# Weights ring of a four-stage transformer trunk: three buffers of 2 MB or six of 1 MB

## Chip, cores, metric

One NeuronCore of a Trainium2 chip runs the whole kernel as one program. The metric is the device time of one execution in microseconds, the median of several. TensorE multiplies; VectorE (DVE), ScalarE (ACT), GpSimd (POOL) and SyncE (SP) work beside it, each with an instruction stream of its own, tied together by semaphores.

## What is computed

Two decoder layers over 256 tokens of width 1024, all in float32. Each layer mixes tokens (a combined input projection, compressed, selected and windowed attention, a short convolution, a retention branch, gates and an output projection) and then mixes channels, with a layer norm after each:

```
for l in range(2):
    x = layer_norm(ALPHA * x + token_mixer(x, ...), ln1_g[l], ln1_b[l])
    f = swiglu(x, ffn_gate, ffn_up, ffn_down) if l == 0 else moe_swiglu(x, router, moe_gate, moe_up, moe_down)
    x = layer_norm(ALPHA * x + f, ln2_g[l], ln2_b[l])

swiglu(x, g, u, d) = (silu(x @ g) * (x @ u)) @ d        # 1024 -> 3584 -> 1024
moe_swiglu: top 2 of 8 experts for each token, softmax over the two logits, each expert a swiglu
```

Every weight is used once per execution, so some 493 MB of them pass through the core.

## The kernel before

**The stream of weights.** The host cuts all large weights into subs of 128 partitions x 2048 floats (1 MB) in the order of their use: 46 subs for a mixer, 42 for the dense layer, 46 for the second mixer and 42 for each of eight experts, 470 in all. Two neighbouring subs make a tile of 2 MB, in which each partition's row of 16 KB is contiguous. `NTILES` is 235. The ring `raw` has `RING` = 3 slots of one tile each. SP fills it (lines 276 to 309): the first three tiles at the start, the constants behind the first, then each tile t when `lo_done` has reached 2t - 4, which is when VectorE has split sub 2t - 5, the second half of the tile that had the slot. One more tile, that nobody reads, is loaded at the end.

**The split.** A float32 product is made of three passes with the shorter type fp32r. ScalarE's `split` (line 823) waits until the tile has landed (`landed`, one semaphore for each slot, only before the even sub) and until TensorE has used the sub three before (`sub_used`), and rounds the sub into `w_hi`, a ring of three subs. VectorE's `split` (line 1114) waits for it and writes the rest, raw - w_hi, to `w_lo` (line 1117) and counts `lo_done`. TensorE waits for `lo_done` of a sub before it multiplies with it. So raw is free after VectorE's split.

**The stages.** Mixers and dense layer run with 256 tokens; their matmuls are recorded at lines 329 to 331 and 343 to 345. For the experts the tokens of one expert are gathered into 128 slots by a matmul with a selection matrix (line 716), and outputs are scattered back (lines 785, 786) and added with the weights on VectorE (line 1589, `add_scattered`). A loop runs over items; an item is an expert, with an extra item for an expert that has more than 128 tokens. In this run there are eight. An item has 42 subs: two for the first gate block, and then per block of 512 hidden channels two for `up`, two for the next `gate`, two for `down` (the last block has no next gate). `body` in each engine's `experts` is one block of six subs, in which each engine has its instructions between the splits by a fixed hand-written order: TensorE multiplies `up`, half of the next gate, makes the four transposes of `hidden` (line 742), multiplies the other half and `down`; ScalarE applies silu (line 1039) and copies the transposed hidden (`hidden_block`, line 1043); VectorE multiplies silu by up (line 1565) and writes its lower part `act_lo` (`lower`, line 1569) between two splits. TensorE's `down` waits for that lower part.

The queue of an engine is in order: a split that waits for its weights holds up all that stands behind it on ScalarE, and through `hi_done` what stands behind the split on VectorE. SP's queue holds only the loads. The norms' parameters (1 MB, line 849, `load_norm`) are loaded by ScalarE's queue.

Of the kernel before, what the change touches and what calls it, by code (L numbers as in the profile page):

```python
# [23 lines left out]
ACT = mybir.ActivationFunctionType  # L24
# [3 lines left out]
P = 128  # L28
D = 1024
# [3 lines left out]
DK = D // P  # L33
# [12 lines left out]
NE = 8  # L46
# [11 lines left out]
LAYER = MIX + FFN  # L58
MOE0 = LAYER + MIX
RING = 3  # L60
NEXT = (0, MIX, LAYER, MOE0)
NTILES = (MOE0 + NE * FFN) // 2
ITEM_TILES = FFN // 2


PA = (0, 1)
# [67 lines left out]
def trunk(nc, wstream, x, consts, constb, small, ln, router, out):  # L134
    with ExitStack() as ctx:
# [4 lines left out]
            return ctx.enter_context(nc.semaphore(name))  # L140


        raw = sb("raw", [P, RING, 2 * SUB])
        w_hi = sb("w_hi", [P, RING, SUB], F32R)
        w_lo = sb("w_lo", [P, RING, SUB], F32R)
        xT_hi = sb("xT_hi", [P, DK, T], F32R)
# [81 lines left out]
        logT = rg[0:NE, 0, :]  # L228


        landed = [sem(f"landed{i}") for i in range(RING)]
        hi_done, lo_done = sem("hi_done"), sem("lo_done")
        sub_used = sem("sub_used")
        half_unit = sem("half_unit")
# [25 lines left out]
            sem(n) for n in ("esilu_rdy", "ehid_rdy", "et_ps", "ehT_hi", "ehT_rdy", "y_hi_rdy", "y_rdy", "scat_ps", "acc_rdy"))  # L260
        act_chain, dve_chain = sem("act_chain"), sem("dve_chain")

        def wait_landed(eng, sub):

            tile = sub // 2
            eng.wait_ge(landed[tile % RING], 16 * (tile // RING + 1))

        def raw_half(slot, half):
            return raw[:, slot, half * SUB:(half + 1) * SUB]

        block = ctx.enter_context(nc.Block())


        @block.sync
        def _(sp):
            sp.dma_start(X[:, :, :], x.rearrange("(t p) d -> p t d", p=P)).then_inc(x_in, 16)
            sp.dma_start(ident, consts[:, C_ID:C_ID + P]).then_inc(x_in, 16)
            for t in range(RING):
                sp.dma_start(raw[:, t], wstream[t]).then_inc(landed[t], 16)
                if t == 0:  # L280
                    sp.dma_start(cst[:, P:C_W], consts[:, P:C_W]).then_inc(const_in, 16)
                    sp.dma_start(cstf, constb).then_inc(const_in, 16)
                    sp.dma_start(sm[:, :, :], small.rearrange("l p c -> p l c")).then_inc(const_in, 16)
            rest = NTILES - RING

            def tile(slot, src, index):

                sp.wait_ge(lo_done, 2 * index - 2 * RING + 2)
                sp.dma_start(raw[:, slot], src).then_inc(landed[slot], 16)

            with sp.Fori(0, rest // RING) as i:
                for c in range(RING):
                    t = i * RING + (RING + c)
                    tile(c, wstream[bass.ds(t, 1)].rearrange("a p c -> (a p) c"), t)
            for t in range(RING + rest // RING * RING, NTILES):
                tile(t % RING, wstream[t], t)

            sp.wait_ge(table_rdy, 1)
            extra = sp.value_load(table[0:1, NX:NX + 1], min_val=0, max_val=NX)
            with sp.If(extra > 0):  # L300
                with sp.Fori(0, extra) as i:
                    e = sp.value_load(table[0:1, bass.ds(i, 1)], min_val=0, max_val=NE - 1)
                    with sp.Fori(0, ITEM_TILES // RING) as b:
                        for c in range(RING):
                            t = e * ITEM_TILES + b * RING + (MOE0 // 2 + c)
                            tile((NTILES + c) % RING, wstream[bass.ds(t, 1)].rearrange("a p c -> (a p) c"),
                                 i * ITEM_TILES + b * RING + (NTILES + c))

            tile(NTILES % RING, wstream[0], extra * ITEM_TILES + NTILES)


        @block.tensor
# [506 lines left out]
        def _(act):  # L819
# [2 lines left out]

            def split(at, k=0):

                if at % 2 == 0:
                    act.wait_ge(landed[at // 2 % RING], (k + (at // 6 + 1)) * 16)
                if at >= RING:
                    act.wait_ge(sub_used, k * 6 + (at - RING + 1))
                activate(w_hi[:, at % RING], raw_half(at // 2 % RING, at % 2), ACT.Copy).then_inc(hi_done, 1)  # L829

            def norm(n):

# [277 lines left out]
        def _(dve):  # L1110
# [3 lines left out]
            def split(at, k=0):  # L1114

                dve.wait_ge(hi_done, k * 6 + (at + 1))
                v.tensor_tensor(w_lo[:, at % RING], raw_half(at // 2 % RING, at % 2), w_hi[:, at % RING],  # L1117
                                ALU.subtract).then_inc(lo_done, 1)

            def add_x(n, t, c):  # L1120
# [524 lines left out]
def host_layout(a):  # L1645

    def rows(w, k):
        return w.reshape(k, P, -1).transpose(1, 0, 2)

    def cut(w, k):  # L1650
        w = rows(w, k)
        n = w.shape[2] // 256
        return w.reshape(P, k, n, 256).transpose(2, 0, 1, 3).reshape(n, P, SUB)

    subs = []
    for l in range(L):
        w = a["w_in"][l]
        q, kv, ng, rest = w[:, :512], w[:, 512:1280], w[:, 1280:1304], w[:, 1304:]
        ngp = np.zeros((D, 256), np.float32)
        ngp[:, :24] = ng  # L1660
        conv_b, conv_c, conv_h = rest[:, :512], rest[:, 512:1024], rest[:, 1024:1536]
        ret, mg = rest[:, 1536:3584], rest[:, 3584:].reshape(D, 3, D)
        first = list(cut(np.concatenate([q, kv, ngp], 1), DK))
        subs += first[:4]
        for kv_ in range(2):
            w1 = a["cmp_w1"][l, kv_].reshape(16, P, CH)
            for h in range(2):
                subs.append(w1[8 * h:8 * h + 8].transpose(1, 0, 2).reshape(P, SUB))
        subs += first[4:]
        subs += list(cut(np.concatenate([conv_c, conv_h, conv_b, ret], 1), DK))  # L1670
        for b in (1, 0, 2):
            g = cut(mg[:, b], DK)
            br = [rows(a["w_br"][l, b][:, c * 512:(c + 1) * 512], 4).reshape(P, SUB) for c in range(2)]
            subs += [g[0], g[1], br[0], g[2], g[3], br[1]]
        for c in range(2):
            wo = rows(a["w_out"][l][:, c * 512:(c + 1) * 512], DK)
            subs += [wo[:, 4 * h:4 * h + 4].reshape(P, SUB) for h in range(2)]
        if l == 0:
            gate, up, down = a["ffn_gate"][0], a["ffn_up"][0], a["ffn_down"][0]
            g, u = cut(gate, DK), cut(up, DK)  # L1680
            d = down.reshape(2 * NB, 2, P, D).transpose(0, 2, 1, 3).reshape(2 * NB, P, SUB)
            subs += [g[0], g[1]]
            for b in range(NB):
                subs += [u[2 * b], u[2 * b + 1]]
                if b + 1 < NB:
                    subs += [g[2 * b + 2], g[2 * b + 3]]
                subs += [d[2 * b], d[2 * b + 1]]
    head = np.stack(subs).reshape(-1, 2, P, SUB).transpose(0, 2, 1, 3).reshape(-1, P, 2 * SUB)
    stream = np.empty((NTILES, P, 2 * SUB), np.float32)
    stream[:len(head)] = head  # L1690
    assert len(head) == MOE0 // 2
    t = len(head)

    def wide(w):
        return rows(w, DK).reshape(P, DK, NB, 512).transpose(2, 0, 1, 3).reshape(NB, P, 2 * SUB)
    for e in range(NE):
        g, u = wide(a["moe_gate"][0, e]), wide(a["moe_up"][0, e])
        d = a["moe_down"][0, e].reshape(NB, 4, P, D).transpose(0, 2, 1, 3).reshape(NB, P, 2 * SUB)
        stream[t] = g[0]
        t += 1  # L1700
        for b in range(NB):
            stream[t] = u[b]
            t += 1
            if b + 1 < NB:
                stream[t] = g[b + 1]
                t += 1
            stream[t] = d[b]
            t += 1
    assert t == NTILES

    small = np.zeros((L, P, S_W), np.float32)
    for l in range(L):
        s = small[l]
        for kv in range(2):
            s[:, S_POS + kv * P:S_POS + kv * P + 16] = a["cmp_pos"][l, kv].reshape(16, P).T
        s[:, S_B1:S_B1 + 4] = a["cmp_b1"][l].reshape(4, P).T
        w2 = a["cmp_w2"][l].reshape(2, 2, P, DH)
        for c in range(2):
            s[:, S_W2K + c * P:S_W2K + c * P + DH] = w2[0, c]
            s[:, S_W2K + c * P + DH:S_W2K + (c + 1) * P] = w2[0, c]  # L1720
            s[:, S_W2V + c * DH:S_W2V + (c + 1) * DH] = w2[1, c]
        s[:DH, S_B2K] = a["cmp_b2"][l, 0]
        s[DH:, S_B2K] = a["cmp_b2"][l, 0]
        s[:, S_CONV:S_CONV + 12] = a["conv_w"][l].reshape(12, P).T
        s[:, S_GNG:S_GNG + 4] = a["ret_gn_g"][l].reshape(4, P).T
        s[:, S_GNB:S_GNB + 4] = a["ret_gn_b"][l].reshape(4, P).T
        s[0, S_B2V:S_B2V + DH] = a["cmp_b2"][l, 1]
    ln = np.stack([np.stack([a[f"ln{n}_g"][l], a[f"ln{n}_b"][l]]) for l in range(L) for n in (1, 2)])
    router = np.zeros((P, DK, P), np.float32)
    router[:, :, :NE] = rows(a["moe_router"][0], DK)  # L1730
    return stream, small, ln, router
# [49 lines left out]
```

## Time and profile before

| | us |
|---|---|
| median of 3 runs | 1923.12 (1921.77 to 1929.84) |
| profiled execution, its own time | 1928.55 |
| its span, first to last instruction | 1926.7 |
| TensorE busy | 1870.9 (97%) |
| VectorE busy | 1429.5 (74%) |
| ScalarE busy | 1131.1 (59%) |
| weights' loads, 236 of 2048 KB, median from issue to landing | 8.9 |

The profile is of one execution. Busy time of TensorE overlaps, since matmuls are pipelined: a matmul of 512 columns is recorded with 0.39 us while the next starts 0.23 us after it. "Idle before" and a wait name the instruction that ended the idle time. In a table of stretches, DMA is the mean busy share of the core's 16 DMA engines in the stretch and GB/s what they moved. Time from issue to landing counts from the instruction on the issuing queue to the last of 16 completions.

### The profile page before, as it was taken

How to read it: one execution, taken by the hardware profiler on the slowest of the kernel's cores; microseconds unless marked ns; L12 is line 12 of the kernel's file. 1: busy time of each engine (PE TensorE's matmuls, PEld its weight loads, DVE VectorE, ACT ScalarE, POOL GpSimd, SP SyncE). 2: the span in 40 equal slices, each digit the busy share in tenths (PEclk: the TensorE clock that was granted, in tenths of full speed). 3: DMA queues.
4: the chain of work that ended last, by engine and by line, in shares of the span. 5: the costliest groups of instructions: out<-in, count | busy, mean ns of one | idle time of the engine just before them, and what ended most of it. 6: DMA issues, size and time to landing. Idle time of an engine off the chain costs nothing.

```text
span 1926.7 us, 28135 instructions
## 1 busy us (share of the span) xinstructions
PE 1870.9 (97%) x11156; PEld 1630.9 (85%) x11160; DVE 1429.5 (74%) x1214; ACT 1131.1 (59%) x972; POOL 0.2 (0%) x4
## 2 busy tenths in 40 slices
PE   7999999999999999999999999999999999999996
PEld 7999998999979999996888888887887887888885
DVE  4585577444565575668888889888888898888987
ACT  5444344443435445435777777777777777776774
POOL 0000000000000000000000000000000000000000
PEclk9999999999999999999999999999999999999998
DMA  8543434554436443454998999989989899899893
GB/s 327 182 167 133 154 140 188 181 202 185 174 131 224 153 149 132 154 186 153 353 364 329 359 345 354 368 321 360 361 327 367 328 363 362 318 366 366 333 369 153
DMA packets 36026, 504.68 MB, mean 262 GB/s; under 512 B 3968, under 2 KB 4096, under 8 KB 5248
## 3 DMA queue, kind: packets, MB, share of 16 engines
q1 hardware_dynamic: 34960, 498.06, 68.9%
q10 hardware_dynamic: 1008, 5.77, 0.8%
q8 instruction: 46, 0.75, 0.2%
q14 instruction: 12, 0.10, 0.0%
HBM read 502.76 MB, written 1.05 MB: 261 GB/s over the span
## 4 chain that ended last, share of the span: by engine, by line
PE 65%; DMA 14%; DVE 10%; ACT 6%; issue 5%; SPq 0%; DVEq 0%; ACTq 0%
DMA raw<-wstream 14%; PE PS L329 10%; PE PS L330 10%; PE PS L331 10%; PE PS L343 9%; PE PS L345 9%; PE PS L344 9%; DVE w_lo L1117 5%; ACT w_hi L829 5%; PE PS L483 1%; PE PS L716 1%; PE PS L742 1%; PE PS L515 1%; DVE act_lo L1569 1%; PE PS L498 1%
## 5 line engine op out<-in xcount | busy, mean ns | idle before, releaser
L1117 DVE TENSOR_TENSOR w_lo<-raw,w_hi 128x2048 fp32r<-128x2048 f32 x472 | 1076.9, 2289 | 346.8 <-ACT w_hi L829 346.2
L829 ACT ACTIVATE w_hi<-raw 128x2048 fp32r<-128x2048 f32 x472 | 902.2, 1915 | 360.0 <-PE PS L345 188.7
L329 PE MATMUL PS<-xT_hi,w_hi 128*128 128x256 f32 x1456 | 421.3, 289 | 10.8 <-DVE w_lo L1117 5.6
L330 PE MATMUL PS<-xT_lo,w_hi 128*128 128x256 f32 x1456 | 414.4, 285 | 0.0
L331 PE MATMUL PS<-xT_hi,w_lo 128*128 128x256 f32 x1456 | 414.2, 284 | 0.0
L343 PE MATMUL PS<-w_hi,xT_hi 128*128 128x512 f32 x896 | 355.1, 396 | 2.6 <-DVE xT_lo L1555 1.5
L345 PE MATMUL PS<-w_hi,xT_lo 128*128 128x512 f32 x896 | 349.6, 390 | 0.0
L344 PE MATMUL PS<-w_lo,xT_hi 128*128 128x512 f32 x896 | 349.0, 390 | 0.0
L329 PEld LDWEIGHTS PS<-xT_hi,w_hi 128*128 128x128 f32 x1456 | 281.8, 194 | 22.7 <-issue 19.7
L330 PEld LDWEIGHTS PS<-xT_lo,w_hi 128*128 128x128 f32 x1456 | 281.9, 194 | 0.2
L331 PEld LDWEIGHTS PS<-xT_hi,w_lo 128*128 128x128 f32 x1456 | 281.7, 193 | 0.0
L343 PE MATMUL PS<-w_hi,act_hi 128*128 128x512 f32 x624 | 246.1, 394 | 12.4 <-DVE act_lo L1569 10.1
L345 PE MATMUL PS<-w_hi,act_lo 128*128 128x512 f32 x624 | 243.1, 390 | 0.0
L344 PE MATMUL PS<-w_lo,act_hi 128*128 128x512 f32 x624 | 243.1, 390 | 0.0
L343 PEld LDWEIGHTS PS<-w_hi,xT_hi 128*128 128x128 f32 x896 | 168.3, 188 | 39.2 <-DVE w_lo L1117 4.5
L345 PEld LDWEIGHTS PS<-w_hi,xT_lo 128*128 128x128 f32 x896 | 168.2, 188 | 35.9
L344 PEld LDWEIGHTS PS<-w_lo,xT_hi 128*128 128x128 f32 x896 | 168.4, 188 | 33.2
L343 PEld LDWEIGHTS PS<-w_hi,act_hi 128*128 128x128 f32 x624 | 117.1, 188 | 45.5 <-DVE w_lo L1117 14.4
L345 PEld LDWEIGHTS PS<-w_hi,act_lo 128*128 128x128 f32 x624 | 117.1, 188 | 24.7
L344 PEld LDWEIGHTS PS<-w_lo,act_hi 128*128 128x128 f32 x624 | 117.2, 188 | 23.3
L911 ACT ACTIVATE G<-PS 128x512 f32<-128x512 f32 x24 | 14.3, 597 | 77.5 <-PE PS L331 40.2
L329 PE MATMUL PS<-act_hi,w_hi 128*128 128x256 f32 x192 | 55.2, 288 | 0.0
(248 smaller groups left out, 1355.1 us busy)
## 6 DMA issues: line engine op xcount, KB each, us to landing
raw<-wstream SPq DMA_DIRECT2D x236, 2048.0 KB, 8.9
soft<-ln ACTq DMA_DIRECT2D x4, 1024.0 KB, 6.5
X<-x SPq DMA_DIRECT2D x1, 1024.0 KB, 4.9
out<-X ACTq DMA_DIRECT2D x2, 512.0 KB, 2.7
cst<-consts SPq DMA_DIRECT2D x1, 890.5 KB, 10.7
sm<-small SPq DMA_DIRECT2D x1, 729.0 KB, 12.5
bufA<-router ACTq DMA_DIRECT2D x1, 512.0 KB, 3.8
rg<-constb SPq DMA_DIRECT2D x1, 335.0 KB, 11.1
```

Source lines behind the costliest of these rows:

```text
L329: mm(o, wh, rhs_hi[:, k, :], start=(k == 0), stop=False)
L330: mm(o, wh, rhs_lo[:, k, :], start=False, stop=False)
L331: last = mm(o, wl, rhs_hi[:, k, :], start=False, stop=(k == nk - 1))
L343: mm(o, lh, wh, start=(first and n == 0), stop=False)
L344: mm(o, lh, wl, start=False, stop=False)
L345: last = mm(o, ll, wh, start=False, stop=(final and n == len(ks) - 1))
L483: last = mm(o[par][:, i, 0:w], query(NR * g + 2 * i + par, qt), kT[par * DH:(par + 1) * DH, a, g, 0:w], start=False, stop=(i == 1), skip_g ...
L498: last = nc.tensor.transpose(PS[:, TB + kb, r * P:(r + 1) * P], prob[:, r, kb * P:(kb + 1) * P], ident)
L515: last = mm(o[par], V[:, a, kb, g * DH:(g + 1) * DH], probT[:, kb * 512 + par * 256:kb * 512 + (par + 1) * 256], start=(a == 0 and kb == 0 ...
L716: last = mm(PS[:, TB + k // 4, (k % 4) * P:(k % 4 + 1) * P], X[:, t, k * P:(k + 1) * P], pick[:, t, :], start=(t == 0), stop=(t == TT - 1))
L829: activate(w_hi[:, at % RING], raw_half(at // 2 % RING, at % 2), ACT.Copy).then_inc(hi_done, 1)
L1117: v.tensor_tensor(w_lo[:, at % RING], raw_half(at // 2 % RING, at % 2), w_hi[:, at % RING], ALU.subtract).then_inc(lo_done, 1)
```

## The change

`raw` becomes a ring of `RAW` = 6 slots of one sub (the same 48 KB of each partition). The host's stream is laid out by subs, each with contiguous rows of 8 KB. SP loads each sub by itself, sub s when `lo_done` has reached s - 5, which is when VectorE has split sub s - 6. The first six subs are loaded at the start, with the constants behind the second. There are six `landed` semaphores, and ScalarE waits for one before each sub. Two subs, not one tile, are loaded at the end for nobody. For the experts the halves of each block are cut so that each sub holds what its half of the tile held. `wait_landed` and `raw_half` go away; the first had no caller.

```
-        raw = sb("raw", [P, RING, 2 * SUB])
+        raw = sb("raw", [P, RAW, SUB])
...
-            for t in range(RING):
+            for t in range(RAW):
                 sp.dma_start(raw[:, t], wstream[t]).then_inc(landed[t], 16)
-                if t == 0:
+                if t == 1:
...
-            def tile(slot, src, index):
-                sp.wait_ge(lo_done, 2 * index - 2 * RING + 2)
+            def load(slot, src, index):
+                sp.wait_ge(lo_done, index - RAW + 1)
                 sp.dma_start(raw[:, slot], src).then_inc(landed[slot], 16)
-            with sp.Fori(0, rest // RING) as i:
-                for c in range(RING):
-                    t = i * RING + (RING + c)
-                    tile(c, wstream[bass.ds(t, 1)].rearrange("a p c -> (a p) c"), t)
+            with sp.Fori(0, rest // RAW) as i:
+                for c in range(RAW):
+                    t = i * RAW + (RAW + c)
+                    load(c, wstream[bass.ds(t, 1)].rearrange("a p c -> (a p) c"), t)
...
-            tile(NTILES % RING, wstream[0], extra * ITEM_TILES + NTILES)
+            for c in range(2):
+                load((NSUBS + c) % RAW, wstream[c], extra * FFN + (NSUBS + c))
...
             def split(at, k=0):        # ScalarE
-                if at % 2 == 0:
-                    act.wait_ge(landed[at // 2 % RING], (k + (at // 6 + 1)) * 16)
+                act.wait_ge(landed[at % RAW], (k + (at // RAW + 1)) * 16)
                 if at >= RING:
                     act.wait_ge(sub_used, k * 6 + (at - RING + 1))
-                activate(w_hi[:, at % RING], raw_half(at // 2 % RING, at % 2), ACT.Copy).then_inc(hi_done, 1)
+                activate(w_hi[:, at % RING], raw[:, at % RAW], ACT.Copy).then_inc(hi_done, 1)
...
             def split(at, k=0):        # VectorE
                 dve.wait_ge(hi_done, k * 6 + (at + 1))
-                v.tensor_tensor(w_lo[:, at % RING], raw_half(at // 2 % RING, at % 2), w_hi[:, at % RING],
+                v.tensor_tensor(w_lo[:, at % RING], raw[:, at % RAW], w_hi[:, at % RING],
                                 ALU.subtract).then_inc(lo_done, 1)
```

## Rows read from the trace of the kernel before

**Rows 1.** Table of stretches: us, each engine's busy time, PEclk, DMA share, GB/s

```profile
1016.30:1772.90 756.60, 747.55 (x3445) 614.23 (x3444) 655.86 (x408) 552.64 (x378) 0.00 (x0) 1.00 0.93 349
1772.90:1897.40 124.50, 123.86 (x575) 102.47 (x574) 109.23 (x68) 92.28 (x63) 0.00 (x0) 1.00 0.92 349
0.00:895.10 895.10, 868.75 (x6524) 806.78 (x6528) 539.14 (x627) 390.50 (x462) 0.20 (x4) 0.99 0.48 176
```

**Rows 2.** Waits (total, times, longest): 895 to 1905, 0 to 895, SP's queue

```profile
ACT w_hi L829 <- DMA raw<-wstream: 88.3, 62, 2.6
PEld PS L343 <- DVE w_lo L1117: 18.9, 25, 1.2
PE PS L343 <- DVE act_lo L1569: 10.1, 23, 1.1
...
ACT w_hi L829 <- DMA raw<-wstream: 6.5, 2, 6.1
...
SPq L289 <- DVE w_lo L1117: 1726.9, 233, 24.6
```

**Rows 3.** Timeline of the start, SP's queue and ScalarE: start, us, instruction

```profile
1.72 0.42 SPq L279 DMA_DIRECT2D raw<-wstream  x1
2.18 0.43 SPq L281 DMA_DIRECT2D cst<-consts  x1
...
8.32 2.06 ACT L845 ACTIVATE xT_hi<-PS 128x512 fp32r<-128x512 f32 x4
10.70 3.71 ACT L829 ACTIVATE w_hi<-raw 128x2048 fp32r<-128x2048 f32 x2 [0.30 <-DMA raw<-wstream]
20.55 1.91 ACT L829 ACTIVATE w_hi<-raw 128x2048 fp32r<-128x2048 f32 x1 [6.15 <-DMA raw<-wstream]
```

**Rows 4.** Timeline of TensorE: first transpose of hidden in six blocks

```profile
1184.96 0.27 PE L742 MATMUL PS<-cst,tmp 128*128 128x128 f32 x1
1201.77 0.27 PE L742 MATMUL PS<-cst,tmp 128*128 128x128 f32 x1
1218.56 0.27 PE L742 MATMUL PS<-cst,tmp 128*128 128x128 f32 x1
1235.76 0.27 PE L742 MATMUL PS<-cst,tmp 128*128 128x128 f32 x1
...
1758.33 0.27 PE L742 MATMUL PS<-cst,tmp 128*128 128x128 f32 x1
1798.08 0.27 PE L742 MATMUL PS<-cst,tmp 128*128 128x128 f32 x1
```

**Rows 5.** Table of stretches: after the start, dense layer, inside an expert

```profile
16.00:28.00 12.00, 12.00 (x95) 12.00 (x94) 6.14 (x4) 4.31 (x3) 0.00 (x0) 1.00 1.02 431
350.00:550.00 200.00, 200.00 (x1412) 188.63 (x1411) 96.34 (x59) 80.48 (x60) 0.00 (x0) 1.00 0.52 189
1452.70:1511.00 58.30, 57.53 (x260) 46.71 (x259) 50.27 (x29) 43.31 (x28) 0.00 (x0) 1.00 0.96 364
```

**Rows 6.** Timeline of ScalarE and VectorE in a disturbed block

```profile
1217.05 1.92 ACT L829 ACTIVATE w_hi<-raw 128x2048 fp32r<-128x2048 f32 x1 [1.82 <-DMA raw<-wstream]
1219.00 2.29 DVE L1117 TENSOR_TENSOR w_lo<-raw,w_hi 128x2048 fp32r<-128x2048 f32 x1 [0.84 <-ACT w_hi L829]
```

**Rows 7.** The tile raw, loads issued in 1452 to 1511 and 1787 to 1825

```profile
DMA to landing us min/median/max: 9.2/9.9/10.1
...
DMA to landing us min/median/max: 7.5/7.7/8.1
```

**Rows 8.** Timeline of an easy stretch: SP's issue of a tile, ScalarE's split of it

```profile
1797.34 0.33 SPq L289 DMA_DIRECT2D raw<-wstream  x1
1806.91 1.92 ACT L829 ACTIVATE w_hi<-raw 128x2048 fp32r<-128x2048 f32 x1 [0.79 <-PE PS L345]
```

**Rows 9.** DMA queues (MB, share of 16 engines): 225 to 240, 320 to 330

```profile
q10 hardware_dynamic: 144, 1.05, 16.6%
...
q10 hardware_dynamic: 144, 1.05, 27.6%
```

More of the change, by code:

```diff
@@ L60 @@
 RING = 3
+RAW = 6
 NEXT = (0, MIX, LAYER, MOE0)
-NTILES = (MOE0 + NE * FFN) // 2
-ITEM_TILES = FFN // 2
+NSUBS = MOE0 + NE * FFN
 PA = (0, 1)
@@ L228, in trunk @@
         logT = rg[0:NE, 0, :]
-        landed = [sem(f"landed{i}") for i in range(RING)]
+        landed = [sem(f"landed{i}") for i in range(RAW)]
         hi_done, lo_done = sem("hi_done"), sem("lo_done")
@@ L261, in trunk @@
         act_chain, dve_chain = sem("act_chain"), sem("dve_chain")
[L263 to L269, printed above, removed]
         block = ctx.enter_context(nc.Block())
@@ L283, in _ @@
                     sp.dma_start(sm[:, :, :], small.rearrange("l p c -> p l c")).then_inc(const_in, 16)
-            rest = NTILES - RING
-            def tile(slot, src, index):
-                sp.wait_ge(lo_done, 2 * index - 2 * RING + 2)
+            rest = NSUBS - RAW
+            def load(slot, src, index):
+                sp.wait_ge(lo_done, index - RAW + 1)
                 sp.dma_start(raw[:, slot], src).then_inc(landed[slot], 16)
-            with sp.Fori(0, rest // RING) as i:
-                for c in range(RING):
-                    t = i * RING + (RING + c)
-                    tile(c, wstream[bass.ds(t, 1)].rearrange("a p c -> (a p) c"), t)
-            for t in range(RING + rest // RING * RING, NTILES):
-                tile(t % RING, wstream[t], t)
+            with sp.Fori(0, rest // RAW) as i:
+                for c in range(RAW):
+                    t = i * RAW + (RAW + c)
+                    load(c, wstream[bass.ds(t, 1)].rearrange("a p c -> (a p) c"), t)
+            for t in range(RAW + rest // RAW * RAW, NSUBS):
+                load(t % RAW, wstream[t], t)
             sp.wait_ge(table_rdy, 1)
@@ L302, in _ @@
                     e = sp.value_load(table[0:1, bass.ds(i, 1)], min_val=0, max_val=NE - 1)
[L303 to L307, printed above, removed]
-            tile(NTILES % RING, wstream[0], extra * ITEM_TILES + NTILES)
+                    with sp.Fori(0, FFN // RAW) as b:
+                        for c in range(RAW):
+                            t = e * FFN + b * RAW + (MOE0 + c)
+                            load((NSUBS + c) % RAW, wstream[bass.ds(t, 1)].rearrange("a p c -> (a p) c"),
+                                 i * FFN + b * RAW + (NSUBS + c))
+            for c in range(2):
+                load((NSUBS + c) % RAW, wstream[c], extra * FFN + (NSUBS + c))
         @block.tensor
@@ L1687, in host_layout @@
                 subs += [d[2 * b], d[2 * b + 1]]
[L1688 to L1692, printed above, removed]
+    assert len(subs) == MOE0
+    stream = np.empty((NSUBS, P, SUB), np.float32)
+    stream[:MOE0] = subs
+    t = MOE0
     def wide(w):
-        return rows(w, DK).reshape(P, DK, NB, 512).transpose(2, 0, 1, 3).reshape(NB, P, 2 * SUB)
+        return rows(w, DK).reshape(P, 2, DK // 2, NB, 512).transpose(3, 1, 0, 2, 4).reshape(NB, 2, P, SUB)
     for e in range(NE):
         g, u = wide(a["moe_gate"][0, e]), wide(a["moe_up"][0, e])
-        d = a["moe_down"][0, e].reshape(NB, 4, P, D).transpose(0, 2, 1, 3).reshape(NB, P, 2 * SUB)
-        stream[t] = g[0]
-        t += 1
+        d = a["moe_down"][0, e].reshape(NB, 2, 2, P, D).transpose(0, 1, 3, 2, 4).reshape(NB, 2, P, SUB)
+        order = [g[0]]
         for b in range(NB):
[L1702 to L1709, printed above, removed]
+            order += [u[b], g[b + 1], d[b]] if b + 1 < NB else [u[b], d[b]]
+        for two in order:
+            stream[t:t + 2] = two
+            t += 2
+    assert t == NSUBS
     small = np.zeros((L, P, S_W), np.float32)
```

## The prediction

> **What bounds the kernel now.** I read three things in this order: the table of stretches with the engines' busy time and the DMA share, the waits, and then single instructions in the stage where the weights can be late. The reader should see two kernels in one. Up to 895 us (mixers, dense layer) the DMA engines are busy 0.48 of the time at 176 GB/s, while TensorE has 868.8 us of 895.1 [rows 1]. In that part the scalar engine waits for weights only twice, 6.5 us in all [rows 2], and 6.15 us of that is one wait at 20.55 us [rows 3], while TensorE runs without an idle moment from 16 to 28 us [rows 5]. So nothing in the first 895 us hangs on the ring but the very first split.
>
> From 895 us on, the eight experts run, one item of the loop each. Over items two to seven the DMA share is 0.93 at 349 GB/s, and TensorE is busy too, 747.5 us of 756.6 [rows 1]. The scalar engine waits 88.3 us for the weights in 62 waits, but most of it is cover: it then waits less for TensorE. What reaches TensorE is 18.9 us of weight loads waiting for the vector engine's split and 10.1 us of matmuls waiting for `act_lo`, which the vector engine writes between splits [rows 2]. Since matmuls overlap, only part of those 29 us is lost. So the stage is bound by TensorE, with small losses where a tile lands late. The DMA engines are nearly full, so the question is both how much is lost and whether smaller transfers keep up.
>
> **How much is lost.** The starts of the four transposes of `hidden` mark the blocks of six subs. Undisturbed blocks take 1201.77 - 1184.96 = 16.81 and 1218.56 - 1201.77 = 16.79 us; the next, in which the weights were late, took 1235.76 - 1218.56 = 17.20 [rows 4]. In a disturbed block one sees the scalar engine's split at 1217.05 wait 1.82 us for the DMA, which pushes the vector engine's split to 1219.00 and the write of `act_lo` behind it [rows 6]. An item without such losses is the first block, 17.3 (it has the scatter's additions on the vector engine), four blocks of 16.8, and the last block with the border of the item, best seen as 1798.08 - 1758.33 = 39.75 [rows 4]: 124.2 us. Items two to seven have 756.6 together [rows 1], 126.1 on average, which is 11.4 over six times 124.2. The eighth (124.5 [rows 1]) has 0.3 more. The first is shorter by what lies before its loop, and I estimate 1.2 for it, three late blocks like that of rows 4. Sum: 12.9 us can be had at the experts. Against the best item alone (124.5) it would be 9.6, the lower bound; if the best border too contains 0.4 us of lateness in each item it is some 16, the upper one.
>
> **Part 1: each 1 MB is refilled when its own split is done.** Tile t (subs 2t and 2t+1) now waits for the split of sub 2t-5. After the change sub s waits for sub s-6. For the odd sub that is the same moment, for the even sub it is one sub, about 2.8 us (a sixth of 16.8), earlier; and the even sub no longer waits for the second MB behind it, 2.5 us at full stream (below). Now: in the disturbed stretch a tile needs 9.2 to 10.1 us from issue to landing, in an easy one 7.5 to 8.1 [rows 7]. The room is read from an easy stretch: the tile issued at 1797.34, right after the split of sub 433, is split from 1806.91 (sub 438), 9.6 us later, with no wait for the DMA [rows 8]. So the room is used up. After: 9.6 + 2.8 = 12.4 us for a transfer half the size. That is 2.8 us more room and 2.5 us less need. The losses above should go, and with them all of the 12.9; the first block's stay, they are in the 17.3.
>
> **Part 2: twice as many transfers of half the size.** 472 splits need 472 transfers of 128 rows of 8 KB, where 236 of 16 KB stood. I price the engines' time of 1 MB as DMA share x bytes / rate. Under a deep queue: 1.02 x 1.049 / 431 = 2.48 us [rows 5]. In the disturbed experts: 0.96 x 1.049 / 364 = 2.77 per MB, 5.53 per tile [rows 5]. In the dense layer, where each tile meets an idle queue: 0.52 x 2.097 / 189 = 5.77 per tile [rows 5]. So a tile has a start cost of about 0.6 (some queue) to 0.8 us (idle queue) above the stream, and next to none in a deep queue. The nearest rows to the new transfer are the norm's loads, 1 MB in 128 rows of 8 KB: alone 27.6% of 10 us = 2.76 us of each engine, and queued behind a tile 16.6% of 15 us = 2.49 [rows 9]. They read one broadcast row and the new ones don't, so I keep both sources. TensorE asks for 1 MB every 124.2 / 42 = 2.96 us. At 0.96 of the time usable [rows 5] that leaves 2.84 us: a start cost of up to 0.36 is free. By the norm's row, alone (0.28) it is free; by the tile's (0.6 to 0.8) it isn't, but then transfers pile up, and a pile is just what takes the cost away [rows 5, 9]. The ring allows a pile: 12.4 us of room against 2.5 of stream and at most 10.1 - 5.0 = 5.1 of everything else that a tile now pays (start, the tile ahead of it, stragglers [rows 7]). So at least 4.8 us, nearly two more transfers, may stand ahead. I take 0 on the path; the bounds are 0 and the slow rival below.
>
> A page of the Trainium skill speaks against the change. "DMA: Bandwidth & Descriptors", section Bandwidth, gives 341 GB/s for a 1 MB transfer and 425 for 16 MB, and asks for at least 1 MB. This trace has 431 GB/s with tiles queued and 364 with one tile behind another [rows 5], so size alone doesn't set it here. At the page's 341 GB/s an item would take 44.04 MB / 341 = 129.2 us, 3.1 more than now in each of eight: 1923 + 25 = 1948 by the page.
>
> **Part 3: the rest.** Issues: 0.33 to 0.42 us each on SP's queue [rows 3, 8], which waited 1726.9 us for the splits [rows 2]; 236 more cost nothing, and nothing else is queued there. Waits: the scalar engine waits for `landed` before each split, not each second one. Behind it stand its split and, behind that, the drains of PSUM. The odd sub's data is issued at the same moment as before, so it comes no later; 236 satisfied waits on an engine that is busy 92 of 124.5 us [rows 1] I take as nothing (bounds: 0 and 236 x 0.04 = 9 us, if none were covered; 0.04 is an estimate from the gap between two issues, 2.18 - 1.72 - 0.42, in rows 3). Start: raw's first MB lands some 2.5 us earlier, but the scalar engine is busy until 10.38, so its split starts 0.3 us earlier [rows 3]; the constants stand behind the same 2 MB as before. The end doesn't change. Matmuls, splits and bytes stay.
>
> **Sum.** 12.9 + 0.3 = 13.2 us against the profiled execution's own 1928.55 (span 1926.7), so 1915.3. That execution lies 5.4 above the median of the three runs, 1923.12. If these 5.4 are themselves late weights, an unprofiled run has only 13.2 - 5.4 = 7.8 to give; if they are something else, all 13.2, and 16 if the upper bound holds. I take the middle of 7.8 and 13.2 and half a microsecond for the upper bound: 11.0, so 1912.1, with a range of its own of 1907 to 1915.5.
>
> **Rivals.** A: the forecast, late weights vanish: 1912.1.
>
> B: the piles are what TensorE already sees. The start cost stays near 0.4 per MB, the engines reach 2.48 + 0.4 over 0.96 = 3.0 us per MB = 126 us per item, just as now. For it: the transfers now already follow each other in the disturbed stretch and still pay 0.57 per tile [rows 5]. Against it: both 1 MB rows of rows 9. Time: 1917 to 1925.
>
> C: the start cost is paid in full by every transfer, whatever stands ahead of it. Then 1 MB costs 2.48 + 0.6 = 3.08, over 0.96 = 3.2 us, so 135 us per item, 9 more than now in each of eight: 1923 + 72 = 1995; with 0.36 us as the point from which it decides and 1940 its near end. The page's 341 GB/s falls in this case. Against it stand the stretch of queued tiles at 431 GB/s and the queued norm load [rows 5, 9].
>
> D: the change doesn't move waits as said. The bytes in flight hardly grow, and the losses have another source, the vector engine's own order (`act_lo` behind a split). Then 1922 to 1924. Against it: the undisturbed blocks have the same order and no loss [rows 4].
>
> **How the numbers follow.** A 0.62, B 0.19, C 0.10, D 0.09. The range reaches from A's low end, 1907, to B's slow end, 1925; it leaves out C and a little of each end. A measurement can tell about 0.5%, 9.6 us: faster means below 1913.5. Of A, 0.44 lies below that and 0.18 above it; B and D are the same, but 0.01 for a B that piles up further. Faster 0.44, same 0.45, slower 0.11.
>
> **What would show it.** Right: items of 124.2 to 124.6 us each, the scalar engine's waits for the DMA in the experts nearly gone (from 88 to under 15 us), its waits for TensorE longer, landing of 1 MB in 5 to 9 us, and the mean rate at 355 GB/s. B shows items of 126 with waits for the DMA still at 50 or more. C shows items above 130, every split of the experts waiting for the DMA, and a DMA share of 0.95 or more at 340 GB/s or less. Wrong altogether: a difference in the first 895 us, or TensorE's granted clock below 1.00 in the experts, where it is 1.00 now [rows 1].

## The result, and the profile after

The changed kernel takes 1910.51 us (1909.42 to 1910.79, 4 runs) against 1925.79 us (1921.77 to 1929.84, 4 runs) of the kernel before: 15.3 us less, a ratio of 0.993 with the interval 0.991 to 0.996. Run again beside the experiments it took 1911.26. Its profiled execution has 1910.68 us and a span of 1908.9.

The table of stretches of the changed kernel (us, busy time of TensorE, its weight loads, VectorE, ScalarE, GpSimd, granted clock, DMA share, GB/s); the stretches are the first 895 us, items two to seven, and the eighth:

```profile
1014.60:1756.80 742.20, 741.34 (x3446) 615.39 (x3445) 655.48 (x408) 554.42 (x378) 0.00 (x0) 1.00 0.94 356
1756.80:1880.50 123.70, 123.56 (x576) 102.56 (x575) 109.26 (x68) 92.40 (x63) 0.00 (x0) 1.00 0.91 345
0.00:894.90 894.90, 868.81 (x6524) 807.05 (x6528) 539.20 (x627) 390.41 (x462) 0.20 (x4) 0.99 0.49 176
```

Against [rows 1]: the six items fall from 756.6 to 742.2 us, that is 123.7 each, and the eighth from 124.5 to 123.7. The first 895 us lose 0.2. With the first item (895.1 to 1016.3 before, 894.9 to 1014.6 after) the experts give 1.5 + 14.4 + 0.8 = 16.7 of the 17.8 us between the two spans. The remaining 0.9 lies behind the eighth item (29.3 to 28.4 us). It isn't the change's: from the last transposes of `hidden` to the end the kernel before has 43.3 us, the changed one 42.5, and the changed one run again 43.2.

The waits of the changed kernel from 895 to 1905 us (total, times, longest), the longest one of ScalarE's split and all that reaches TensorE's weight loads and matmuls at this line from the vector engine's splits:

```profile
ACT w_hi L821 <- PE PS L338: 176.5, 258, 2.2
PEld PS L336 <- DVE w_lo L1109: 4.5, 8, 0.6
```

There is no row any more for ScalarE waiting for the weights in the experts, where it was 88.3 us in 62 waits, nor one for TensorE waiting for `act_lo` at this line (10.1 us in 23 before), and the 18.9 us in 25 waits of the weight loads have become 4.5 in 8 [rows 2]. Eight is one for each item: the first block with the scatter's additions, as the last experiment shows. ScalarE's split now waits for TensorE, which is the healthy sign here: the supplier stands ready and the consumer sets the pace.

The transposes of `hidden` in TensorE's timeline, the answer to [rows 4]; the last pair spans the last block of one item and its border with the next:

```profile
1675.51 0.27 PE L735 MATMUL PS<-cst,tmp 128*128 128x128 f32 x1
1692.32 0.27 PE L735 MATMUL PS<-cst,tmp 128*128 128x128 f32 x1
1709.11 0.27 PE L735 MATMUL PS<-cst,tmp 128*128 128x128 f32 x1
...
1742.72 0.27 PE L735 MATMUL PS<-cst,tmp 128*128 128x128 f32 x1
1781.96 0.27 PE L735 MATMUL PS<-cst,tmp 128*128 128x128 f32 x1
```

Blocks are 16.81 and 16.79 us. Every item has four of these and a first one of 17.2 to 17.3, where many blocks of before had 17.2 to 17.9. The stretch over a border is 1781.96 - 1742.72 = 39.24, where the best one of before had 39.75.

An even sub's way in the timeline, SP's issue and ScalarE's split of it (the answer to [rows 8]):

```profile
1801.19 0.33 SPq L281 DMA_DIRECT2D raw<-wstream  x1
1813.51 1.92 ACT L821 ACTIVATE w_hi<-raw 128x2048 fp32r<-128x2048 f32 x1 [0.80 <-PE PS L338]
```

The tile raw's time from issue to landing, in the experts (1000 to 1870 us) and in the dense layer (350 to 550):

```profile
DMA to landing us min/median/max: 4.7/6.8/8.3
...
DMA to landing us min/median/max: 4.7/4.8/5.1
```

The room is 1813.51 - 1801.19 = 12.3 us, and 8.3 is the most that a transfer needs. Before, the room of an even sub was 9.6 and a tile needed 7.5 to 10.9 in the experts, as the first row of the next section shows.

### The profile page after: what moved, and what is told of

Read it like the earlier page. It is cut to its first block, busy times and chain, and to the rows that moved or that the text cites. A ratio compares the mean times of both kernels' runs of the same rounds, so it can differ in the third digit from the quotient of the medians.

```text
span 1908.9 us, 29045 instructions
## 1 busy us (share of the span) xinstructions
PE 1863.5 (98%) x11156; PEld 1632.6 (86%) x11160; DVE 1429.3 (75%) x1214; ACT 1133.3 (59%) x972; POOL 0.2 (0%) x4
## 4 chain that ended last, share of the span: by engine, by line
PE 90%; DVE 5%; ACT 2%; issue 2%; DMA 0%; DVEq 0%; SPq 0%; ACTq 0%
PE PS L336 17%; PE PS L338 17%; PE PS L337 17%; PE PS L322 10%; PE PS L323 10%; PE PS L324 10%; PE PS L709 2%; ACT w_hi L821 2%; DVE w_lo L1109 2%; PE PS L735 1%; PE PS L476 1%; PE PS L508 1%; PE PS L491 1%; PE PS L408 1%; PE PS L407 1%
## 5 line engine op out<-in xcount | busy, mean ns | idle before, releaser
L1035 ACT ACTIVATE act_hi<-PS 128x512 fp32r<-128x512 f32 x56 | 33.5, 599 | 61.9 <-PE PS L735 61.9
```

The costliest lines, as they stand in the source:

```text
L1035: activate(hT_hi, PS[:, YB, :], ACT.Copy).then_inc(ehT_hi, 1)
```

## Experiments

Every experiment was timed against the kernel before on the same chip; its ratio is given with its interval. To read them, three views of the experts (all for 1000 to 1870 us) are used again and again. For the kernel before, the tile raw's time from issue to landing:

```profile
DMA to landing us min/median/max: 7.5/9.6/10.9
```

The table of stretches:

```profile
1000.00:1870.00 870.00, 859.66 (x3967) 706.66 (x3966) 754.54 (x473) 636.96 (x437) 0.00 (x0) 1.00 0.93 350
```

The DMA queue of SP (packets, MB, share of 16 engines):

```profile
q1 hardware_dynamic: 20887, 304.21, 92.6%
```

From the last row the engines' time for one sub of 1 MB (1.049 million bytes) is worked out: 0.926 x 870 us over 304.21 / 1.049 subs = 2.78 us. The changed kernel has 310.12 MB at 93.6%, so 2.75; run again it has 2.73. Differences of 0.02 or 0.03 in this figure are therefore not read as anything.

The theory: a block loses time where landing takes longer than the room, the time between the refill of a buffer and its use; nothing else of the ring matters. The rivals: the size of the transfer itself makes the difference, the pile of queued transfers does, or each transfer pays a start cost.

**The change again.** No edit.

> The changed kernel itself, beside the three variants on the same chip. Items of 123.7 us, no wait for the DMA in the experts, 1910 us.

1911.26 us (0.994, 0.992 to 0.995), items of 123.7, no wait for the DMA in the experts.

**Which half of the change does it?** Three kernels take it apart. In the first, only the size of the transfer is left, with the shorter row that goes with it: both 1 MB of a pair are issued at the tile's old moment and awaited together.

```
-                sp.wait_ge(lo_done, index - RAW + 1)
+                sp.wait_ge(lo_done, index - RAW + 2 - slot % 2)
...
                 act.wait_ge(landed[at % RAW], (k + (at // RAW + 1)) * 16)
+                if at % 2 == 0:
+                    act.wait_ge(landed[(at + 1) % RAW], (k + (at // RAW + 1)) * 16)
```

> Transfers of 1 MB, but both of a pair issued after the split of sub s-5 (as the 2 MB tile was) and both awaited before the even sub. Only the size of a transfer is left of the change. If the earlier refill and the single landing make the gain: 1922 to 1930, items near 126 us, 50 to 90 us of waits for the DMA. If the size itself makes it (shorter start cost, 1 MB rows of 8 KB): 1910 to 1914. If each transfer paid a start cost of its own: above 1930.

1915.74 us (0.996, 0.994 to 0.997). Between the two expectations: of the 12.9 us that the changed kernel gains against the runs of before beside it, size and row length give 8.4. Its waits from 895 to 1905 us:

```profile
ACT w_hi L823 <- DMA raw<-wstream: 33.2, 24, 2.3
PEld PS L336 <- DVE w_lo L1111: 7.8, 12, 0.8
```

The DMA queue of SP (packets, MB, share of 16 engines):

```profile
q1 hardware_dynamic: 42349, 308.40, 90.3%
```

24 late weights in place of 62, and 0.903 x 870 / (308.40 / 1.049) = 2.67 us of the engines for 1 MB, 0.11 less than before. The later one of each pair, which decides, lands after 6.9 us in the median and 9.7 at most (read load by load in this trace), where the tile of before needs 9.6 and 10.9. So the same bytes, asked for at the same moments, come sooner in smaller pieces, and fewer of them are late.

Then the edit of the first line alone (issue in pairs, own landing), and the edit of the last two alone (own issue, landing in pairs):

> Transfers of 1 MB, both of a pair issued after the split of the same sub, as before; but each sub waits for its own landing only. If the even sub's wait for the second MB was what came too late (some 2.5 us of need): the even sub has 9.6 us of room for about 7, so 1910 to 1913. If the earlier issue is needed: 1920 or more.

> Transfers of 1 MB, each issued when its own slot is free, but the even sub waits for both of the pair. If the earlier issue of the even sub alone is enough: 1910 to 1914, because the odd one, issued 9.6 us before the need, lands in about 7 with the even one already gone. If the wait for the second MB is what hurts: 1918 to 1926, with waits for the DMA before even subs.

1911.33 us (0.994, 0.992 to 0.995) and 1911.49 us (0.993, 0.992 to 0.995). Both met the first of their two expectations: items of 123.7 and no wait for the DMA in the experts. Either half of the change is enough once the transfers are of 1 MB: 2.8 us more room, or 2.5 us less to wait for. Together they leave margin, which this kernel doesn't use. The first of the two also shows that the comparison is one of each sub with its own room: its odd subs land as late as 10.2 us, more than the 8.7 to 9.7 us of an even sub's room, and lose nothing, because an odd sub has at least 11.6; its even ones land within 8.3.

**Size of the transfer or length of the row?** In the paired kernel both changed. One kernel keeps transfers of 2 MB, issued and awaited as before, but with 256 rows of 8 KB from the new layout:

```
-                sp.dma_start(raw[:, slot], src).then_inc(landed[slot], 16)
+                sp.dma_start(raw[:, slot:slot + 2], src).then_inc(landed[slot], 16)
...
-                    load(c, wstream[bass.ds(t, 1)].rearrange("a p c -> (a p) c"), t)
+                    load(c, wstream[bass.ds(t, 2)].rearrange("a p c -> p a c"), t)
```

> Transfers of 2 MB issued and awaited as in the kernel before, but from the new layout, 256 rows of 8 KB instead of 128 rows of 16 KB. With the paired 1 MB transfers (1915.7) it separates the length of a row from the size of a transfer. If the row's length makes the start cost: 1914 to 1918, DMA time of 2.67 us per MB in the experts. If the size of the transfer does: 1922 to 1926 and 2.77 per MB, as before.

1919.44 us (0.997, 0.996 to 0.998), between the two. Its waits from 895 to 1905 us:

```profile
ACT w_hi L821 <- DMA raw<-wstream: 53.9, 38, 2.8
```

From issue to landing:

```profile
DMA to landing us min/median/max: 7.3/8.1/10.9
```

The DMA queue of SP (packets, MB, share of 16 engines):

```profile
q1 hardware_dynamic: 39741, 306.43, 92.5%
```

The shorter rows bring the median landing from 9.6 to 8.1 us and 6.1 us of time, although the engines still need 0.925 x 870 / (306.43 / 1.049) = 2.75 us per MB. Cutting the transfer in two takes another 0.08 us off the engines' time. Its share of the gain is small and uncertain: 8.4 us against 6.1, each against its own runs of before, with ratios whose intervals overlap (0.994 to 0.997, 0.996 to 0.998). In the dense layer, where each tile meets an idle queue, the median landing is 7.8 us with rows of 16 KB and 7.5 with rows of 8 KB: a lone tile gains only 0.3. So most of the 1.5 us in the experts comes up where transfers stand behind each other. Why was not settled.

The other corner keeps rows of 16 KB and halves the transfer by partitions, in the kernel before:

```
-                sp.dma_start(raw[:, slot], src).then_inc(landed[slot], 16)
+                for h in range(2):
+                    rows_ = slice(h * P // 2, (h + 1) * P // 2)
+                    sp.dma_start(raw[rows_, slot], src[rows_]).then_inc(landed[slot], 16)
```

> The kernel before, with each 2 MB tile loaded by two transfers of 64 partitions x 16 KB, issued one behind the other and awaited together. If the row's length makes the start cost: 1922 to 1926, 2.77 us per MB. If the size of the transfer does: 1914 to 1918, 2.67 per MB.

2584.63 us (1.342, 1.339 to 1.345). Both expectations were wrong, and the run says nothing on rows or sizes in transfers of 128 partitions, because it met something larger. The table of stretches:

```profile
1000.00:1870.00 870.00, 642.73 (x2399) 498.05 (x2398) 457.19 (x283) 375.25 (x262) 0.00 (x0) 0.86 1.01 212
```

The DMA queue of SP (packets, MB, share of 16 engines):

```profile
q1 hardware_dynamic: 14095, 184.81, 100.8%
```

All 16 engines are busy all the time (1.01) and move 212 GB/s: 1.008 x 870 / (184.81 / 1.049) = 4.98 us per MB, twice the 2.48 of the full stream [rows 5].

**Room against landing, in steps.** The changed kernel, with each refill one, two or three splits later; the ring behaves as one of five, four and three subs:

```
-                sp.wait_ge(lo_done, index - RAW + 1)
+                sp.wait_ge(lo_done, index - RAW + 2)      # one later; + 3 and + 4 for two and three
```

> The changed kernel with each refill one split later, for all subs (as with a ring of five): room of 9.6 us instead of 12.4, landing now 6.7 on average, 8 at most. Theory (what counts is room against landing): nothing is late, 1910 to 1912. If it is the pile of queued transfers that makes them cheap, a smaller pile gives late weights: 1915 or more.

> Each refill two splits later (as with a ring of four): room of 6.8 us. A transfer to an idle queue lands in 4.8, one behind another in 6.7 or more. Theory: now the losses return, of the size of those before or above: 1920 to 1940, and the DMA waits of the scalar engine in nearly every block. If transfers to an idle queue suffice: 1911 to 1914.

> Each refill three splits later (as with a ring of three subs): room of 4 us, less than the 4.7 of the quickest landing. Room against landing says that every sub of the experts is late by at least 0.7 us: items of 42 x (2.95 + 0.7 to 2.5), so 1990 to 2150 in all, the dense layer slower too or not, since its subs take 5.4 us there. If only the pile counted: the same time as with two splits later.

| refill | room (shortest and median, read from issue and split of each sub) | landing in the experts, min/median/max | ScalarE's waits for the DMA there | time | ratio |
|---|---|---|---|---|---|
| as changed | 11.6, 12.4 | 4.7/6.8/8.3 | none | 1911.26 | 0.994 |
| one later | 8.7, 9.7 | 4.7/6.7/8.2 | none | 1912.39 | 0.993 (0.991 to 0.995) |
| two later | 5.7, 6.9 | 4.7/5.6/7.9 | 51.1 us, 52 | 1924.91 | 1.001 (0.999 to 1.003) |
| three later | 4.7, 4.9 | 4.6/4.8/6.7 | 256.4 us, 252 | 2005.58 | 1.041 (1.040 to 1.043) |

The waits of the last one, from 895 to 1905 us:

```profile
ACT w_hi L821 <- DMA raw<-wstream: 256.4, 252, 2.1
```

The rule holds in all four: nothing is lost while the shortest room is above the latest landing (8.7 above 8.2), the first losses come where they cross (5.7 and 6.9 within 4.7 to 7.9), and with a room as short as the quickest landing the scalar engine waits at 252 of 336 subs: items of 135.4 us. The time with three later lies in the range that I gave, but the reasoning was off: with every sub late by 0.7 us or more an item would have been 153 us. The room of 4 us that I expected is 4.9, since a late ring also stretches the time between splits, and the 256 us of waits lengthened the eight items by some 94 in all (135.4 against 123.7), not by their full length.

The single runs lie between 1921 and 1937 with two later, between 1909 and 1912 with none later, and between 2003.7 and 2006.5 with three later, which has by far the most late weights. So runs don't differ simply by how much is late; they differ most where the room lies among the landing times. That chance decides there which weights are late is an inference, since each kernel has one trace.

**Do small transfers pay a start cost each?** Each sub in two transfers of 512 KB:

```
+                for h in range(2):
+                    cols = slice(h * SUB // 2, (h + 1) * SUB // 2)
-                sp.dma_start(raw[:, slot], src).then_inc(landed[slot], 16)
+                    sp.dma_start(raw[:, slot, cols], src[:, cols]).then_inc(landed[slot], 16)
...
-                act.wait_ge(landed[at % RAW], (k + (at // RAW + 1)) * 16)
+                act.wait_ge(landed[at % RAW], (k + (at // RAW + 1)) * 32)
```

> The changed kernel with each sub loaded by two transfers of 512 KB (128 rows of 4 KB), issued one behind the other, at the same moments as now. If the start cost is one for each moment of issue, not for each transfer (the paired 1 MB transfers had 2.67 us per MB where single ones have 2.75): no more than 2.8 us per MB, nothing late, 1910 to 1912. If each transfer pays 0.25 us or more: 3.0 per MB, items of 126 or more, 1925 to 1950.

1910.26 us (0.992, 0.990 to 0.994), items of 123.7. The table of stretches, in the experts and in the full stream of the start:

```profile
1000.00:1870.00 870.00, 868.99 (x4037) 721.71 (x4037) 768.12 (x480) 650.60 (x444) 0.00 (x0) 1.00 0.97 357
16.00:28.00 12.00, 12.00 (x87) 12.00 (x86) 5.80 (x4) 4.31 (x3) 0.00 (x0) 0.83 1.03 409
```

The DMA queue of SP (packets, MB, share of 16 engines):

```profile
q1 hardware_dynamic: 85188, 310.20, 96.9%
```

0.969 x 870 / (310.20 / 1.049) = 2.85 us per MB, a little above the 2.8 of the better expectation. Four transfers for 2 MB where the kernel before has one cost 0.07 us per MB of the engines' time and nothing on the path. The halved transfers also have halved rows, and the full stream from 16 to 28 us hints that the rows are what costs: rows of 16 KB run there at 431 GB/s [rows 5], rows of 8 KB at 420 to 423 both in transfers of 2 MB and of 1 MB, rows of 4 KB at 409. From 420 to 409 is 2.52 to 2.63 us per MB (share 1.007 and 1.022 of the 16 engines), the same 0.1 as from 2.75 to 2.85 in the experts. Transfers of 512 KB with rows of 8 KB were not tried.

**What is left.** TensorE's remaining waits inside the items are the eight of the first block, and ScalarE loads its table late at the start. Two edits on the changed kernel:

```
-                        if c == 3 and item is not None:
-                            add_scattered(item, (2, 3))
+                        if c in (3, 5) and item is not None:
+                            add_scattered(item, (2 + (c == 5),))
...
             act.wait_ge(const_rdy, 1)
+            activate(rstd[:, 0:1], eps[:, :], ACT.Copy)
             norm(0)
```

> The changed kernel with two small edits where TensorE still waits: VectorE's two additions of the scattered output in the first block of an item stand before the third and the fifth split instead of together before the third, and ScalarE's first activation (with its table load of 1.28 us) is a copy of one column before the first transposes are there. Expected: items of 123.4 instead of 123.7 (8 x 0.3 = 2.4 us) and a start 1.3 us earlier: 1907. If the additions then hold up the split that follows the fifth place: items stay at 123.7, and only the start is gained, 1909.

1906.80 us (0.990, 0.988 to 0.992), some 4 us below the changed kernel (its runs lie between 1905.3 and 1908.0, those of the changed kernel between 1909.3 and 1911.9), and the fastest version. Its stretch:

```profile
1000.00:1870.00 870.00, 870.00 (x4054) 724.90 (x4053) 771.35 (x481) 652.27 (x446) 0.00 (x0) 1.00 0.93 358
```

TensorE is busy 870.0 of 870.0 us; an item takes 123.25, 0.46 less than 123.71, or 3.7 us over eight, where 0.3 an item was expected. The start gave only 0.3 us in place of 1.3: the table is there at 2.0, but the transposes that feed the first copies end as before, and so the first split starts at 10.01 instead of 10.28.

## Why the prediction was right or wrong

**The place: right.** The gain is in the experts and in TensorE's waits there; the first 895 us changed by 0.2.

**The sum: the mechanism right, one term too small.** 12.9 us were to be had at the experts, with bounds of 9.6 and 16; between the two profiled executions it was 16.7. The floor of an item was built from 17.3, four times 16.8 and the best border of the trace, 39.75. The blocks were right to 0.05, the border was not: it is 39.24 without late weights. The best of the seven borders still contained 0.5 us, and 0.5 in each of eight items is the 4 that the sum missed. I had named this as the upper bound, with 0.4. No border of before's trace was undisturbed as a whole, so the minimum was no floor. But its two parts were there, each in some item: from the sixth block's transposes to the seventh's 15.84 us at best, from the seventh's to the next item's first ones 23.39. Their sum is 39.23, the border as measured after. The start was put at 0.3 and its first matmul moved by 0.4 (15.08 to 14.68), half of which is gone by 895 us.

**From the profile to the median.** I halved the doubt on the 5.4 us by which the profiled execution lay above the median of three. The kernel before has 1919.9 to 1929.8 over its 33 runs in this study, 1925.4 in their middle, the changed one 1909.3 to 1911.9 over eight. That the spread of before was late weights fits this, but no second trace of before was taken to show it; 1923.12 lay in the lower half of the spread. The forecast of 11.0 us against 1923.12 gave 1912.1; measured 1910.5, and the gain against runs taken beside it 12.9 to 15.3. So the time was hit more closely than the gain, and part of that is luck: against 1925.79, the median with the fourth run, the forecast gain is 4.3 too small, and the low 1923.12 hid 2.7 of it.

**Part 1.** Room of 12.4 us: 12.3 in the row above. Of it, landing takes 8.3 at most, so 4.1 us are left where the prediction had at least 4.8: the latest landing holds more beside its own stream than the 5.1 read from [rows 7]. Both halves of part 1 (earlier issue, own landing) were counted together; each is enough. What I missed is that landing itself shrinks for the same bytes at the same moments: two thirds of the gain came with the size and the row's length, before any refill was earlier.

**Part 2.** A start cost of up to 0.36 us per MB would be free: measured 2.75 - 2.48 = 0.27, or 0.25 when run again. The reason given, that a pile takes the cost away, holds in direction: the same transfers of 1 MB stand 0.44 above the stream in the dense layer, where each meets an idle queue (52.6% of 200 us for 37.75 MB, so 2.92), 0.36 in the experts with each refill three splits later (87.5% of 870 us for 281.40 MB, so 2.84), and 0.26 to 0.28 with two, one or none later. So some overlap lowers it, more overlap changes nothing, and part of it stays: the pile doesn't bring it down to 0, and the norm's single transfers (0.28 alone) understated it. By size it is 0.30 per MB at 2 MB, 0.27 at 1 MB and 0.37 at 512 KB: it does not go with the count of transfers. Only issuing 1 MB transfers in pairs lowered it (0.19 and 0.18 in the two kernels that do). The 0.6 us for every transfer, on which rival C stood, was not there: from 1 MB to 512 KB the cost rose by 0.1 per MB, which the shorter rows may account for.

**The Trainium skill's rule** ("DMA: Bandwidth & Descriptors", section Bandwidth: 341 GB/s at 1 MB) would, by the estimate in the prediction, have made an item 129.2 us. This trace does not agree: the transfers of 1 MB ran at 356 GB/s and those of 512 KB at 357, in both cases because TensorE asked for no more; in the full stream of the start 1 MB transfers reach 420. With a refill that is late three times over, the same size fell to 323 with the engines' share at 0.88. The page's figure is of transfers issued from GpSimd, and whether they overlap isn't told; here, from SP's queue, the overlap decides.

**The rivals.** B (items of 126, waits of 50 us) and C (items above 130) didn't happen: items of 123.7, below even the 124.2 to 124.6 that the forecast gave as its sign, and no waits. D, the vector engine's own order, was not the source of before's losses, but its order is what is left, in another place: the additions in the first block cost 0.46 us in each item, which the last experiment took away.

**Part 3.** 236 more issues and 236 more satisfied waits cost nothing that can be seen: the first 895 us, where ScalarE is often next to the path, are 0.2 us shorter.

## What to carry to other kernels

For a ring of buffers compare two numbers from the trace: the room, from a buffer's refill to its use, and the latest landing, not the median one. Take the shortest room, and sub by sub where subs have different rooms. While the room is larger, refilling earlier, splitting the landing or deepening the ring gives nothing; refills one split later, as a ring of five subs would have them, did here. Where they cross, a cure that takes no memory is to cut the transfer so that refill and landing go by the piece that is consumed; down to 512 KB the pieces cost 0.1 us of the engines per MB here, with one transfer in flight behind another.

To build a floor from the best stretches of a trace, ask whether the best one was ever undisturbed, and cut a long stretch into short pieces: each piece is more likely to have been undisturbed once. And when runs of a kernel spread by several us, as those of the kernel before and with refills two splits later did, look whether a room lies among the landing times.

## What the runs showed of the hardware that was not expected

Transfers of 64 partitions x 16 KB ran at half the rate of those of 128 partitions: 212 GB/s with all 16 DMA engines at 1.01, 4.98 us per MB against 2.48. Two of them, one for each half of the partitions, stood in the queue one behind the other and did not fill in for each other: even to the idle queue of the dense layer the quickest half landed after 7.2 us and the latest after 13.2, where 1 MB in 128 partitions takes 4.7 to 5.1. The Trainium skill ("DMA: Bandwidth & Descriptors", section Rules for kernel authors) says not to bother with two transfers to disjoint partition halves, because they go one after the other on the same engines; the trace shows more than that, a loss of half the rate. Which part is shared was not tried.

The same bytes in rows of 8 KB instead of 16 KB, in transfers of the same size, landed 1.5 us sooner in the median (8.1 against 9.6) in the experts, where transfers follow each other closely, and 0.3 sooner (7.5 against 7.8) in the dense layer, where the queue is idle. In the full stream of the start the longer rows were the faster ones: 431 GB/s against 420.
